# Normalisation sums by quarters of the tokens, and the hand-over from the experts to the second block, in a two-block transformer kernel

## Chip, cores and metric

The kernel runs on one core of a Trainium2 chip. The metric is the device time of one execution in microseconds (us). TensorE multiplies matrices, VectorE (DVE), ScalarE (ACT) and GpSimd (POOL) work element by element, SyncE (SP) issues the transfers from memory.

## What is computed

Two blocks, on 256 latent tokens and 256 context tokens of 1024 features, all in fp32:

```python
def first_block(x, c, ctx, ...):
    hl, hc = modulate(x, ...), modulate(ctx, ...)
    s_f, s_b = ssd_context_states(hc, lp)             # a state-space mixer, both directions
    out, _, _ = mix_stream(hl, lp, True, s_f, s_b)    # its output goes through rms_norm_gated
    x = post_norm(x, gate * out, ...)
    return post_norm(x, gate2 * hier_moe(modulate(x, ...)), ...)     # 32 experts, 2 for each token

def second_block(x, c, ctx, ...):
    for l in range(2):
        x, ctx   = post_norm_2(x, 0.5 * g1 * swiglu_2(modulate_2(x, ...))), ...     # f1i0, f1i1
        x, ctx   = post_norm_2(x, g2 * mixer(...)), ...    # l = 0: gla and latent attention; 1: neighbourhood attention
        x, ctx   = post_norm_2(x, 0.5 * g3 * swiglu_2(modulate_2(x, ...))), ...     # f2i0, f2i1

def layer_norm_2(x):
    mu = mean(x, -1);  var = mean(square(x - mu), -1)
    return (x - mu) * rsqrt(var + EPS)

def rms_norm(x, g):
    return x * rsqrt(mean(square(x), -1) + EPS) * g
```

The context is carried along until the mixer of l = 1; from there on only the 256 latent tokens are.

## The kernel before

**Layout.** Features lie on the 128 partitions, tokens along the free dimension. X is [128, 8, 512]: eight tiles of 128 features by 512 tokens, context in columns 0 to 255 and latent tokens in 256 to 511. A sum over features is thus a sum over partitions and over eight tiles, and TensorE does it: `onesD` is a 128 x 128 matrix of 1/1024, and eight fp32 matmuls against the tiles, accumulated in one PSUM bank, give the mean of each token on all 128 partitions.

**Linear layers.** Weights and inputs are split into a rounded high part and a rest (`HR`, `LR` of a weight tile `RAW`; `AH`, `AL` of an input), and a product is three matmuls: AH*HR, AL*HR, AH*LR. A weight tile is 128 x 2048 and comes through a ring of three slots; ScalarE rounds it and DVE takes the rest (`cut`). A second matrix of a feed-forward layer has its inputs in `BH`, `BL` (`BHf1i`, `BHf2i`). `linear_pe` runs the layer, output tile by output tile, and calls `after(m)` behind tile m.

**A norm.** `residual_dve` adds output tile m, times a gate, to X. `mean_pe` puts the sum of X's tile m-1 into the layer behind its output tile m; the last two sums stand behind the layer. Then come `norm_dve` (subtract the mean, eight tiles; wait for the root; reciprocal; multiply), `norm_act` (square, eight tiles; root of the variance) and `norm_pe` (eight sums of the squares, into bank 6). Behind the multiplication the lead (`lead_act`, `lead_dve`) makes AH and AL of the next layer: ScalarE applies scale and shift into `tmp` and rounds it, DVE takes the rest. The next layer's first matmul waits for the first tile of both. This form stands seven times: `out1` (256 tokens, before the routing), f1i0, `eout` (even mixer), f2i0 and f1i1 (512 tokens), `nout` (odd mixer) and f2i1 (256 tokens). ScalarE's square root needs a table load, which the program has directly behind the squares.

**Behind the experts.** The expert stage is one of two branches (`few`, at most 17 experts in use, or `every`), and its end is `after_pe`, `after_act`, `after_dve`. ScalarE waits for the context's transfer (`ctx2`), scales, shifts and rounds eight context tiles and then rounds two weight tiles (`cut(1)` takes slots 0 and 1), and only then squares for the norm `out2`. DVE adds the experts' output to X (eight), takes eight rests of the context and two of weights, and then centres. The norm's eight mean sums come with nothing beside them on TensorE.

**Small norms.** In `merge` the squares of the gated output are summed inside the z layer (16 sums, 256 tokens), and `rz`, root and reciprocal, is multiplied in 16 and more tiles later. In the even mixer the linear attention (`gla`) normalises each of four heads by a sum of one tile of 512 tokens (`omean`), and the latent attention's two inputs `ck` and `cq` (1 and 3 tiles) are normalised likewise (`cmean`), with one buffer for the squares.

**What sets the order.** Each engine has a program written out by hand, one function for each stage and engine (`ffn_act`, `gla_pe`), and does its instructions in that order. They wait for one another by named ticks on semaphores. PSUM banks are given out in order (`T.bank`) or by number (`T.hold`), and taken again when the reader frees them.

## Time and profile before

| | |
|---|---|
| median of 3 runs | 3360.7 us (3357.94 to 3367.04) |
| profiled execution | 3353.11 us |
| its span, first to last record | 3351.3 us |
| TensorE matmuls busy | 3049.3 us, 91% |
| TensorE weight loads busy | 2355.9 us, 70% |
| DVE busy | 1418.5 us, 42% |
| ScalarE busy | 1078.4 us, 32% |
| GpSimd busy | 308.4 us, 9% |
| mean granted TensorE clock | 0.959 |
| moved | 537.27 MB, mean 160 GB/s |

The rows further down come from one profiled execution. In the profile PE is TensorE, L188 the line that issues every matmul and L194 that of the transposes, L313 every ScalarE operation. Rows read "output<-inputs", buffer numbers left out; `ar`, `arf1i` and `arf2i` are the stages' scratch memories, in which squares, roots and `tmp` lie. One fp32 matmul appears as two records. Matmul records overlap, so a price is read from start to start. The chain is followed back from the last instruction, each step to what released it.

### The profile page before, as it was taken

How to read it: one execution, taken by the hardware profiler on the slowest of the kernel's cores; microseconds unless marked ns; L12 is line 12 of the kernel's file. 1: busy time of each engine (PE TensorE's matmuls, PEld its weight loads, DVE VectorE, ACT ScalarE, POOL GpSimd, SP SyncE). 2: the span in 40 equal slices, each digit the busy share in tenths (PEclk: the TensorE clock that was granted, in tenths of full speed). 3: DMA queues.
4: the chain of work that ended last, by engine and by line, in shares of the span. 5: the costliest groups of instructions: out<-in, count | busy, mean ns of one | idle time of the engine just before them, and what ended most of it. 6: DMA issues, size and time to landing. Idle time of an engine off the chain costs nothing.

```text
span 3351.3 us, 43646 instructions
## 1 busy us (share of the span) xinstructions
PE 3049.3 (91%) x18814; PEld 2355.9 (70%) x18814; DVE 1418.5 (42%) x2096; ACT 1078.4 (32%) x1579; POOL 308.4 (9%) x309
## 2 busy tenths in 40 slices
PE   6988898889999979999887888999989999897998
PEld 4866698855555548787676556878768787773998
DVE  4665454522222243333576454333243333436554
ACT  4443353312222242222432233222242121434443
POOL 0024370200000010000113001000010000300000
PEclk9988899889999989999999899999999999999999
DMA  7567755489999933232349121222222323310453
GB/s 225 161 198 234 233 163 147 150 330 396 390 391 391 398 108 97 82 109 68 94 132 319 46 76 63 91 87 95 86 82 85 104 78 98 128 62 1 138 177 101
DMA packets 415213, 537.27 MB, mean 160 GB/s; under 512 B 14340, under 2 KB 389924, under 8 KB 390308
## 3 DMA queue, kind: packets, MB, share of 16 engines
q1 hardware_dynamic: 415012, 534.38, 46.5%
q8 instruction: 151, 2.47, 0.3%
q14 instruction: 50, 0.41, 0.0%
HBM read 533.30 MB, written 1.05 MB: 159 GB/s over the span
## 4 chain that ended last, share of the span: by engine, by line
PE 82%; DVE 8%; ACT 5%; DMA 3%; issue 2%; SPq 0%; POOL 0%; DVEq 0%; ACTq 0%; POOLq 0%
PE ps L188 80%; PE ps L187 2%; DVE ar L243 2%; ACT ar L313 2%; DMA RAW<-in_ada_w 1%; DVE LR L243 1%; DVE ar L259 1%; ACT HR L313 1%; DMA RAW<-in_w_in 1%; PE ps L194 1%; DVE ar L253 0%; DVE ar L249 0%; DVE ar L262 0%; ACT arf1i L313 0%; ACT AH L313 0%
## 5 line engine op out<-in xcount | busy, mean ns | idle before, releaser
L188 PE MATMUL ps<-AH,HR 128*128 128x512 f32 (+1 forms) x2552 | 900.4, 353 | 63.3 <-DVE AL L243 40.0
L188 PE MATMUL ps<-AL,HR 128*128 128x512 f32 (+1 forms) x2552 | 886.7, 347 | 0.0
L188 PE MATMUL ps<-AH,LR 128*128 128x512 f32 (+1 forms) x2552 | 885.8, 347 | 0.0
L243 DVE TENSOR_TENSOR LR<-RAW,HR 128x2048 fp32r<-128x2048 f32 (+3 forms) x232 | 485.9, 2096 | 596.2 <-ACT HR L313 593.6
L313 ACT ACTIVATE HR<-RAW 128x2048 fp32r<-128x2048 f32 (+3 forms) x232 | 404.1, 1744 | 765.8 <-PE ps L188 664.3
L188 PEld LDWEIGHTS ps<-AH,HR 128*128 128x128 f32 x2552 | 490.1, 192 | 135.6 <-ACT arf1i L313 19.9
L188 PEld LDWEIGHTS ps<-AL,HR 128*128 128x128 f32 x2552 | 490.4, 192 | 60.0 <-issue 1.9
L188 PEld LDWEIGHTS ps<-AH,LR 128*128 128x128 f32 x2552 | 489.7, 192 | 58.9
L249 POOL TENSOR_SCALAR X<-X 128x512 f32<-128x512 f32 (+2 forms) x50 | 83.7, 1700 | 2239.7 <-ACT AH L313 1629.2
L188 PE MATMUL ps<-ar 64*128 64x128 f32 (+9 forms) x1318 | 233.5, 366 | 59.7 <-ACT ar L313 26.8
L188 PEld LDWEIGHTS ps<-ar 64*128 64x128 f32 (+2 forms) x1318 | 137.7, 186 | 137.8 <-issue 44.9
L253 DVE SCALAR_TENSOR_TENSOR X<-ps,mod,X 128x256 f32<-128x256 f32 x152 | 67.4, 479 | 313.1 <-PE ps L188 313.1
L243 POOL TENSOR_TENSOR ar<-ar 128x384 f32<-128x384 f32 (+5 forms) x138 | 151.9, 1109 | 289.9 <-DVE ar L243 115.3
L313 ACT ACTIVATE ar<-ar 128x384 f32<-128x384 f32 (+7 forms) x208 | 109.4, 557 | 158.2 <-DVE ar L249 53.7
L188 PE MATMUL ps<-BHf1i,HR 128*128 128x512 f32 x352 | 147.9, 420 | 11.6 <-DVE BLf1i L243 11.6
L313 ACT ACTIVATE ar<-ps 128x256 f32<-128x256 f32 (+4 forms) x190 | 89.1, 475 | 198.2 <-PE ps L188 189.7
L188 PE MATMUL ps<-BHf1i,LR 128*128 128x512 f32 x352 | 142.3, 404 | 0.0
L188 PE MATMUL ps<-BLf1i,HR 128*128 128x512 f32 x352 | 142.3, 404 | 0.0
L313 ACT ACTIVATE ar_few<-ps 128x512 f32<-128x512 f32 x64 | 47.0, 734 | 287.2 <-PE ps L188 287.2
L188 PE MATMUL ps<-RAW,CS 128*32 128x128 f32 x3072 | 123.3, 310 | 16.4 <-DMA RAW<-in_ada_w 8.2
L188 PE MATMUL ps<-BHf2i,HR 128*128 128x512 f32 (+1 forms) x352 | 123.6, 351 | 9.6 <-DVE BLf2i L243 9.6
L188 PE MATMUL ps<-BHf2i,LR 128*128 128x512 f32 (+1 forms) x352 | 119.6, 340 | 0.0
(182 smaller groups left out, 3748.8 us busy)
## 6 DMA issues: line engine op xcount, KB each, us to landing
RAW<-in_ada_w SPq DMA_DIRECT2D x72, 1024.0 KB, 6.4
RAW<-in_f1i SPq DMA_DIRECT2D x44, 1024.0 KB, 5.0
RAW<-in_f2i SPq DMA_DIRECT2D x44, 1024.0 KB, 5.1
RAW<-in_w_in SPq DMA_DIRECT2D x32, 1024.0 KB, 5.6
RAW<-in_w_ada SPq DMA_DIRECT2D x24, 1024.0 KB, 8.0
RAW<-in_w_eu SPq DMA_DIRECT2D x17, 1024.0 KB, 10.0
HF<-in_w_ed SPq DMA_DIRECT2D x17, 1024.0 KB, 7.8
LF<-in_w_eu SPq DMA_DIRECT2D x17, 1024.0 KB, 10.1
```

The source lines that it names most:

```text
L187: return self.e.matmul(o, w, x, start=start, stop=stop, skip_group_check=True)
L188: return self.e.matmul(o, w, x, start=start, stop=stop)
L194: return self.e.transpose(o, a, self.K.ident[sp:sp + q, sp:sp + q])
L243: return self.e.tensor_tensor(o, a, b, op) if self.e else NOTHING
L249: return self.e.tensor_scalar(o, a, s1, None, o1)
L253: return self.e.scalar_tensor_tensor(out=o, in0=a, scalar=s, in1=b, op0=o1, op1=o2) if self.e else NOTHING
L259: return self.e.reciprocal(x, x) if self.e else NOTHING
L313: return self.e.activation(o, a, f, **k) if self.e else NOTHING
```

## The change

A sum over features has a new form. `sums_pe` splits the tokens into quarters: quarter g is multiplied by 32 columns of `onesD` (now 128 x 32) into partitions 32g to 32g+31, so four matmuls with 32 weight columns and a quarter of the moving columns take the place of one with 128 columns and all tokens. The result is a 128 x n/4 tile whose row group g holds the means of quarter g. ScalarE copies it, or its root, to `stat` in SBUF, and `spread_pe` brings it back to 128 x n in a PSUM bank: four matmuls with `pick` (one matrix per quarter, with a row of ones in row 32g), one per quarter. Root and reciprocal work on n/4 columns, and DVE multiplies by the spread factor from PSUM. All norms use this, the small ones of gla, the latents and the gated norm too (there ScalarE copies the spread factor to `rz`).

Behind the experts, GpSimd scales and shifts the context into `h32` inside the expert stage (`context_pool`), and ScalarE only rounds it. One weight tile is split (`cut(0)`) in place of two, on ScalarE between the mean's copy and the squares and on DVE between the centring and the reciprocal; of the eight context rests four stand ahead of the centring and four behind. The squares of `out2` have a buffer of their own (`sq2`), `tmp2` has two tiles in place of four. The latents' squares go into `v2`, one place each, with no wait between.

```diff
 
+def sums_pe(T, K, b, x, n, first, last):
+
+    w = n // 4
+    for g in range(4):
+        r = T.mm(b[32 * g:32 * g + 32, 0:w], K.onesD[:, 0:32], x[:, g * w:(g + 1) * w], first, last)
+    return r
+
+
+def spread_pe(T, K, b, x, n):
+
+    w = n // 4
+    for g in range(4):
+        r = T.mm(b[:, g * w:(g + 1) * w], K.pick[:, g, :], x[:, 0:w], True, True)
+    return r
+
+
 def mean_pe(T, K, tag, x, n, bank=7):
 
     T.hi = 7
-    mb, held = T.hold(bank, tag, "mean")
...
         T.wait_ge(*h)
 
     def add(m):
         T.wait_ge(*K.dve.of(tag, "x", m))
-        r = T.mm(mb[:, 0:n], K.onesD[:, :], x[:, m, :], m == 0, m == 7)
+        r = sums_pe(T, K, mb, x[:, m, :], n, m == 0, m == 7)
         if m == 7:
-            r.then_inc(*K.pe(tag, "mean"))
+            r.then_inc(*K.pe(tag, "sums"))
 
...
-    vb, held = T.hold(6, tag, "var")
+    act, dve, pe = K.act, K.dve, K.pe
+    mb, held = T.hold(6, tag, "mean")
+    for h in held:
+        T.wait_ge(*h)
+    T.wait_ge(*act.of(tag, "mean row"))
+    spread_pe(T, K, mb, K.stat, n).then_inc(*pe(tag, "mean"))
+    vb, held = T.hold(7, tag, "var")
     for h in held:
         T.wait_ge(*h)
     for k in range(8):
-        T.wait_ge(*K.act.of(tag, "sq", k))
-        r = T.mm(vb[:, 0:n], K.onesD[:, :], sq[:, k, :], k == 0, k == 7)
-    r.then_inc(*K.pe(tag, "var"))
+        T.wait_ge(*act.of(tag, "sq", k))
+        r = sums_pe(T, K, vb, sq[:, k, :], n, k == 0, k == 7)
+    r.then_inc(*pe(tag, "var"))
+    rb, held = T.hold(6, tag, "factor")
+    for h in held:
+        T.wait_ge(*h)
+    T.wait_ge(*dve.of(tag, "factor row"))
+    spread_pe(T, K, rb, K.stat, n).then_inc(*pe(tag, "factor"))
     T.hi = 8
 
 
-def norm_act(S, K, tag, x, n, eps, sq, rs, post):
+def norm_act(S, K, tag, x, n, eps, sq, post, meanwhile=None):
     pe, dve, act = K.pe, K.dve, K.act
+    row = K.stat[:, 0:n // 4]
+    S.wait_ge(*pe.of(tag, "sums"))
+    S.act(row, K.ps(tag, "sums")[:, 0:n // 4], ACT.Copy).then_inc(*act(tag, "mean row"))
+    K.free(act, tag, "sums")
+    if meanwhile:
+        meanwhile()
     for k in range(8):
         S.wait_ge(*dve.of(tag, "centred", k))
         S.act(sq[:, k, :], x[:, k, :], ACT.Square).then_inc(*act(tag, "sq", k))
     S.wait_ge(*pe.of(tag, "var"))
-    S.wait_ge(*act.last)
-    S.act(rs, K.ps(tag, "var")[:, 0:n], ACT.Sqrt, bias=K.eps[:, eps:eps + 1]).then_inc(*act(tag, "root"))
+    S.act(row, K.ps(tag, "var")[:, 0:n // 4], ACT.Sqrt, bias=K.eps[:, eps:eps + 1]).then_inc(*act(tag, "root"))
     K.free(act, tag, "var")
     for k in range(8):
         post(k)
 
 
-def norm_dve(V, K, tag, x, n, rs, pre, post):
+def norm_dve(V, K, tag, x, n, pre, post, meanwhile=None):
     pe, dve, act = K.pe, K.dve, K.act
     V.wait_ge(*pe.of(tag, "mean"))
     for k in range(8):
         V.tt(x[:, k, :], x[:, k, :], K.ps(tag, "mean")[:, 0:n], SUB).then_inc(*dve(tag, "centred", k))
     K.free(dve, tag, "mean")
+    if meanwhile:
+        meanwhile()
     V.wait_ge(*act.of(tag, "root"))
+    V.rec(K.stat[:, 0:n // 4]).then_inc(*dve(tag, "factor row"))
     V.wait_ge(*dve.last)
-    V.rec(rs).then_inc(*dve())
-    V.wait_ge(*dve.last)
+    V.wait_ge(*pe.of(tag, "factor"))
     for k in range(10):
         if k < 8:
-            V.tt(x[:, k, :], x[:, k, :], rs, MUL).then_inc(*dve(tag, "normed", k))
+            V.tt(x[:, k, :], x[:, k, :], K.ps(tag, "factor")[:, 0:n], MUL).then_inc(*dve(tag, "normed", k))
+            if k == 7:
+                K.free(dve, tag, "factor")
             if pre:
...
+        self.onesD = sb("onesD", [128, 32], F32)
+        self.pick = sb("pick", [128, 4, 128], F32)
+        self.stat = sb("stat", [128, 128], F32)
...
-    for t, v in ((K.onesD[:, :], 1.0 / 1024), (K.ones[:, :], 1.0), (K.eps[:, 0:1], 1e-5), (K.eps[:, 1:2], 1e-6)):
+    for t, v in ((K.onesD[:, :], 1.0 / 1024), (K.ones[:, :], 1.0), (K.eps[:, 0:1], 1e-5), (K.eps[:, 1:2], 1e-6),
+                 (K.pick[:, :, :], 0.0)):
         G.fill(t, v).then_inc(*K.pool("constants"))
+    G.wait_ge(*K.pool.last)
+    for g in range(4):
+        G.fill(K.pick[32 * g:32 * g + 1, g, :], 1.0).then_inc(*K.pool("constants"))
+        G.wait_ge(*K.pool.last)
 
 
 def setup_act(S, K):
...
+    for w in held:
+        T.wait_ge(*w)
+    T.wait_ge(*dve.of("rz row"))
+    spread_pe(T, K, b, K.stat, 256).then_inc(*pe("rz"))
...
-    S.act(o.rz, K.ps("ssq")[:, 0:256], ACT.Sqrt, bias=K.eps[:, 0:1], scale=0.5).then_inc(*act("rz"))
+    S.act(K.stat[:, 0:64], K.ps("ssq")[:, 0:64], ACT.Sqrt, bias=K.eps[:, 0:1], scale=0.5).then_inc(*act("rz root"))
...
+    S.wait_ge(*pe.of("rz"))
+    S.act(o.rz, K.ps("rz")[:, 0:256], ACT.Copy).then_inc(*act("rz"))
+    K.free(act, "rz")
...
-    V.rec(o.rz).then_inc(*dve("rz"))
+    V.wait_ge(*act.of("rz root"))
+    V.rec(K.stat[:, 0:64]).then_inc(*dve("rz row"))
...
 
+def context_pool(G, K):
+
+    m = K.mod2[0]
+    G.wait_ge(K.loaded["ctx2"], 16)
+    for k in range(8):
+        G.ts(K.route.h32[:, k, :], K.X[:, k, 0:256], m[:, 8 + k, 1:2], m[:, k, 1:2], MUL, ADD).then_inc(K.scaled, 1)
+
+
 class Every:
 
 
...
+    context_pool(G, K)
     K.pool.note("end")
 
...
+    context_pool(G, K)
...
+        S.wait_ge(*dve.of("out2", "normed", k))
         if k > 1:
-            S.wait_ge(*dve.of("f1i0h", v, k - 2))
-        tb = K.tmp2[:, i, :]
-        S.act(tb, K.X[:, k, s:s + 256], ACT.Identity, scale=m2[:, 8 + k, v:v + 1],
-              bias=m2[:, k, v:v + 1]).then_inc(*act())
+            S.wait_ge(*dve.of("f1i0h", 0, k - 2))
+        S.act(tb, K.X[:, k, 256:512], ACT.Identity, scale=m2[:, 8 + k, 0:1], bias=m2[:, k, 0:1]).then_inc(*act())
         S.wait_ge(*act.last)
-        S.act(K.AH[:, k * 512 + s:k * 512 + s + 256], tb, ACT.Copy).then_inc(*act("f1i0h", "hi", k))
-        act.note("f1i0h", v, k)
-
-    def post(k):
-        S.wait_ge(*dve.of("out2", "normed", k))
-        half(k, 256, 0, 2 + k % 2)
-
-    for k in range(8):
-        half(k, 0, 1, k % 2)
-    S.cut(1)
-    norm_act(S, K, "out2", o.XL, 256, 0, o.h32, o.rs, post)
+        S.act(K.AH[:, k * 512 + 256:k * 512 + 512], tb, ACT.Copy).then_inc(*act("f1i0h", "hi", k))
+
+    norm_act(S, K, "out2", o.XL, 256, 0, o.sq2, post, lambda: S.cut(0))
     act.note("lead end")
 
 
...
-        half(k, 0, 1, k % 2)
-    V.cut(1)
-    norm_dve(V, K, "out2", o.XL, 256, o.rs, ("ln2g", "ln2b"), lambda k: half(k, 256, 0, 2 + k % 2))
+    def context(k):
+        at = slice(k * 512, k * 512 + 256)
+        V.wait_ge(*act.of("f1i0h", 1, k))
+        V.tt(K.AL[:, at], o.h32[:, k, :], K.AH[:, at].bitcast(F32), SUB).then_inc(*dve("f1i0h", 1, k))
+
+    def meanwhile():
+        for k in range(4, 8):
+            context(k)
+        V.cut(0)
+
+    def latents(k):
+        at = slice(k * 512 + 256, k * 512 + 512)
+        V.wait_ge(*act.of("f1i0h", "hi", k))
+        V.tt(K.AL[:, at], K.tmp2[:, k % 2, :], K.AH[:, at].bitcast(F32), SUB).then_inc(*dve("f1i0h", "lo", k))
+        dve.note("f1i0h", 0, k)
+
+    for k in range(4):
+        context(k)
+    norm_dve(V, K, "out2", o.XL, 256, ("ln2g", "ln2b"), latents, meanwhile)
     dve.note("lead end")
 
...
 
+    def factor(hd):
+        T.wait_ge(*dve.of("ofactor row", hd))
+        spread_pe(T, K, bank("ofactor", hd), o.rss[hd], 512).then_inc(*pe("ofactor", hd))
...
-        T.mm(bank("omean", hd)[:, :], K.onesD[:, :], o.sqs[hd % 2], True, True).then_inc(*pe("omean", hd))
...
+            factor(hd - 1)
+    factor(3)
     pe.note("gla end")
 
...
-        S.act(o.rss[hd % 2], K.ps("omean", hd)[:, :], ACT.Sqrt, bias=K.eps[:, 1:2],
+        S.act(o.rss[hd], K.ps("omean", hd)[:, 0:128], ACT.Sqrt, bias=K.eps[:, 1:2],
               scale=8.0).then_inc(*act("oroot", hd))
...
 
+    def onorm(hd):
+        V.wait_ge(*pe.of("ofactor", hd))
+        then(V.stt(o.oT[:, hd, :], o.oT[:, hd, :], K.v("gng"), K.ps("ofactor", hd)[:, :], MUL, MUL))
+        K.free(dve, "ofactor", hd)
...
-        rs = o.rss[hd % 2]
         V.wait_ge(*act.of("oroot", hd))
...
         if hd < 2:
...
+    onorm(3)
     dve.note("gla end")
...
+        r.then_inc(*pe("cmean", i))
+
+    def factor(i):
+        b = bank("cfactor", i)
+        T.wait_ge(*dve.of("cfactor row", i))
+        spread_pe(T, K, b, o.P[0][:, 128 * i:128 * i + 128], 512).then_inc(*pe("cfactor", i))
+
+    factor(0)
+    factor(1)
     j, w = T.weights("ukv", None, 0, 1, 0, 1024, False)
...
-        if i:
-            S.wait_ge(*dve.of("cnorm", 0))
-        S.act(o.P[0], K.ps("cmean", i)[:, :], ACT.Sqrt, bias=K.eps[:, 1:2], scale=w).then_inc(*act("croot", i))
+            S.act(o.v2[:, i + m, :], x[:, m, :], ACT.Square).then_inc(*act("csq", i, m))
+    for i, w in enumerate((8.0, 1024.0 / 384)):
+        S.wait_ge(*pe.of("cmean", i))
...
 
+    for i in range(2):
+        V.wait_ge(*act.of("croot", i))
...
-        then(V.rec(o.P[0]))
+        V.wait_ge(*pe.of("cfactor", i))
         for m in range(nt):
-            then(V.stt(x[:, m, :], x[:, m, :], K.v(key, m), o.P[0], MUL, MUL), "cnorm", i)
+            then(V.stt(x[:, m, :], x[:, m, :], K.v(key, m), K.ps("cfactor", i)[:, :], MUL, MUL), "cnorm", i)
+        K.free(dve, "cfactor", i)
     V.take()
     for hd in range(4):
```

**ScalarE, from the end of the expert branches to the lead of f1i0.** `tmp` is the context, or the latent tokens, scaled, `ar<-X` the squares and `ar<-ps,eps` the root. Before:

```order
L313 ACTIVATE tmp<-X,mod 128x256
L313 ACTIVATE AH<-tmp 128x256
L313 ACTIVATE HR<-RAW 128x2048 x2
L313 ACTIVATE ar<-X 128x256 x8
L313 ACT_TABLE_LOAD
L313 ACTIVATE ar<-ps,eps 128x256
L313 ACTIVATE tmp<-X,mod 128x256
L313 ACTIVATE AH<-tmp 128x256
```

(The first two rows are the last of eight such pairs.) Now, with `ar` the context as GpSimd has scaled it, and `ar_all<-X` the squares:

```order
L313 ACT_TABLE_LOAD
L313 ACTIVATE AH<-ar 128x256 x8
L313 ACTIVATE stat<-ps 128x64
L313 ACTIVATE HR<-RAW 128x2048
L313 ACTIVATE ar_all<-X 128x256 x8
L313 ACT_TABLE_LOAD
L313 ACTIVATE stat<-ps,eps 128x64
L313 ACTIVATE tmp<-X,mod 128x256
L313 ACTIVATE AH<-tmp 128x256
```

The eight scalings and one weight tile have gone from the front of the squares, and the other weight tile now stands behind the copy of the mean.

**DVE, the same place.** `X<-ps,mod,X` adds the experts' output, `AL` rows are the rests of the context, `X<-X,ps` first the centring. Before:

```order
L253 SCALAR_TENSOR_TENSOR X<-ps,mod,X 128x256 x8
L243 TENSOR_TENSOR AL<-tmp,AH 128x256 x8
L243 TENSOR_TENSOR LR<-RAW,HR 128x2048 x2
L243 TENSOR_TENSOR X<-X,ps 128x256 x8
L259 RECIPROCAL ar<-ar 128x256
L243 TENSOR_TENSOR X<-X,ar 128x256
```

Now:

```order
L253 SCALAR_TENSOR_TENSOR X<-ps,mod,X 128x256 x8
L243 TENSOR_TENSOR AL<-ar,AH 128x256 x4
L243 TENSOR_TENSOR X<-X,ps 128x256 x8
L243 TENSOR_TENSOR AL<-ar,AH 128x256 x4
L243 TENSOR_TENSOR LR<-RAW,HR 128x2048
L259 RECIPROCAL stat<-stat 128x64
L243 TENSOR_TENSOR X<-X,ps 128x256
```

Four rests of the context and the one weight rest have moved behind the centring, the second weight rest is gone from here.

**TensorE, from the last layer rows of f1i0's second matrix to the first of the even mixer.** `arf1i` are the squares, AH*HR begins the next layer. Before:

```order
L188 MATMUL ps<-BHf1i,HR 128x512
L188 MATMUL ps<-BLf1i,HR 128x512
L188 MATMUL ps<-BHf1i,LR 128x512
L188 MATMUL ps<-X,onesD 128x512 x2
L188 MATMUL ps<-arf1i,onesD 128x512 x8
L188 MATMUL ps<-AH,HR 128x512
```

Now:

```order
L188 MATMUL ps<-BHf1i,HR 128x512
L188 MATMUL ps<-BLf1i,HR 128x512
L188 MATMUL ps<-BHf1i,LR 128x512
L188 MATMUL ps<-X,onesD 32x128 x8
L188 MATMUL ps<-stat,pick 128x128 x4
L188 MATMUL ps<-arf1i,onesD 32x128 x32
L188 MATMUL ps<-stat,pick 128x128 x4
L188 MATMUL ps<-AH,HR 128x512
```

Each sum has become four small ones, and two spreads have come in: one between the mean's sums and the squares', one between the squares' and the next layer.

## Rows read from the trace of the kernel before

**Rows 1.** The page, chain that ended last, shares of the span by engine

```profile
PE 82%; DVE 8%; ACT 5%; DMA 3%; issue 2%; SPq 0%; POOL 0%; DVEq 0%; ACTq 0%; POOLq 0%
```

**Rows 2.** Chain, behind f1i0 and even mixer; columns: start us, us, what

```profile
1620.87 1.14 PE ps L188 x2
...
1623.43 7.15 PE ps L188 x16
...
1631.33 3.36 DVE arf1i L259
...
1638.07 19.15 PE ps L188 x72
...
2053.00 8.81 PE ps L188 x16
```

**Rows 3.** Chain, behind the experts

```profile
1210.51 3.23 DVE X L253 x8
...
1219.85 1.81 ACT HR L313
...
1223.96 2.28 DVE LR L243
...
1234.83 0.43 DVE X L243
...
1238.10 6.97 PE ps L188 x17
```

**Rows 4.** Chain, end of linear attention and the latents

```profile
1886.35 0.69 ACT ar L313
...
1896.86 0.64 ACT ar L313
...
1906.50 30.37 PE ps L188 x90
```

**Rows 5.** Timeline, TensorE: start us, us, what; sums inside 512-, then 256-token layers

```profile
1572.46 1.02 PE L188 MATMUL ps<-X,onesD 128*128 128x512 f32 x2
...
1573.55 0.39 PE L188 MATMUL ps<-BLf1i,HR 128*128 128x512 f32 x1
...
627.14 0.59 PE L188 MATMUL ps<-X,onesD 128*128 128x256 f32 x2
...
627.69 0.28 PE L188 MATMUL ps<-AL,HR 128*128 128x256 f32 x1
```

**Rows 6.** Timeline, TensorE, a conditioning job inside a layer

```profile
113.28 1.08 PE L188 MATMUL ps<-RAW,CS 128*32 128x128 f32 x32
...
114.63 0.40 PE L188 MATMUL ps<-AL,HR 128*128 128x512 f32 x1
```

**Rows 7.** Groups of instructions, ScalarE, the copy of a conditioning row

```profile
L313 ACT ACTIVATE mrow<-ps 128x128 f32<-128x128 f32 x96 | 26.2, 273 | 111.6 <-PE ps L188 95.3 <-DMA X<-in_ctxT 16.0
```

**Rows 8.** Timeline, TensorE, transposes in the routing

```profile
664.55 3.31 PE L194 MATMUL ps<-ident,ar 128*128 128x128 f32 x16
```

**Rows 9.** Timeline, ScalarE, table loads behind f1i0 and behind nout

```profile
1627.64 1.28 ACT L313 ACT_TABLE_LOAD   x1
...
3131.23 1.28 ACT L313 ACT_TABLE_LOAD   x1
```

**Rows 10.** Chain, reciprocal of the 256-token norm nout

```profile
3133.30 1.76 DVE ar L259
```

**Rows 11.** DMA issues in 655 to 700 us; last column: us to landing

```profile
X<-in_ctx2T SPq DMA_DIRECT2D x1, 1024.0 KB, 28.1
```

**Rows 12.** Timeline, ScalarE, first weight tile in f1i0

```profile
1248.70 1.92 ACT L313 ACTIVATE HR<-RAW 128x2048 fp32r<-128x2048 f32 x1 [2.33 <-POOL X L249]
```

**Rows 13.** Timeline, ScalarE, roundings for the layer ya

```profile
522.57 4.90 ACT L313 ACTIVATE AH<-ar,vec 128x256 fp32r<-128x256 f32 x12
```

**Rows 14.** Engines by stretch: busy us of PE, PEld, DVE, ACT, POOL; granted clock

```profile
1638.00:1644.00 6.00, 5.93 (x15) 4.74 (x16) 6.00 (x8) 5.87 (x12) 6.00 (x4) 0.54 0.00 0
```

More of the change, by code:

```diff
@@ L1485, in post @@
               bias=mod[:, 24 + k, 0:1]).then_inc(*act("h32", k))
-    norm_act(S, K, "out1", o.XL, 256, 0, o.sq, o.rs, post)
+    norm_act(S, K, "out1", o.XL, 256, 0, o.sq, post)
     for q in range(2):
@@ L1501, in route_dve @@
     meet(V, K, "out1 end")
-    norm_dve(V, K, "out1", o.XL, 256, o.rs, ("ln1g", "ln1b"), None)
+    norm_dve(V, K, "out1", o.XL, 256, ("ln1g", "ln1b"), None)
     for j in range(2):
@@ L2652, in gla_dve @@
             read(hd + 1)
-        rs = o.rss[hd % 2]
         V.wait_ge(*act.of("oroot", hd))
-        then(V.rec(rs))
-        then(V.stt(o.oT[:, hd, :], o.oT[:, hd, :], K.v("gng"), rs, MUL, MUL), "onorm", hd)
-        then(V.tt(o.oT[:, hd, :], o.oT[:, hd, :], o.r[:, hd, :], MUL))
+        V.rec(o.rss[hd]).then_inc(*dve("ofactor row", hd))
         if hd < 2:
@@ L2660, in gla_dve @@
                 pass
+        if hd:
+            onorm(hd - 1)
+    onorm(3)
     dve.note("gla end")
@@ L2888, in latent_dve @@
     meet(V, K, "even out")
-    norm_dve(V, K, "eout", K.X, 512, o.rs, None, lead_dve(V, K, o.lead))
+    norm_dve(V, K, "eout", K.X, 512, None, lead_dve(V, K, o.lead))
     dve.note("even end")
@@ L3010, in odd_act @@
     meet(S, K, "odd out")
-    norm_act(S, K, "nout", o.XL, 256, 1, o.sq, o.rs, lead_act(S, K, o.lead, "nout"))
+    norm_act(S, K, "nout", o.XL, 256, 1, o.sq, lead_act(S, K, o.lead, "nout"))
     act.note("odd end")
@@ L3057, in odd_dve @@
     meet(V, K, "odd out")
-    norm_dve(V, K, "nout", o.XL, 256, o.rs, None, lead_dve(V, K, o.lead))
+    norm_dve(V, K, "nout", o.XL, 256, None, lead_dve(V, K, o.lead))
     dve.note("odd end")
```

71 lines of the change are left out of this document (34 added, 37 removed).

## Prediction

> **What bounds the kernel now.** I read the page's chain of waits first: 82% of the span is TensorE work that follows other TensorE work [rows 1]. The reader is to see there that only two kinds of edit can pay: less work on TensorE inside its dense stages, and shorter hand-overs where it stands still. Then I took the chain, in order of time, around the places that the diff touches. It shows the hand-over of a 512-token norm: last sum of the mean, eight matmuls for the variance, root, reciprocal, first matmul of the next layer, 17.2 us from 1620.87 to 1638.07 [rows 2]. The kernel has four of these (behind f1i0, even mixer, f2i0, f1i1), three for 256 tokens on the path of the same shape (out1, nout, f2i1), a 256-token one behind the experts with more work ahead of it [rows 3], and the small norms at the end of the linear attention [rows 4]. The matmuls of the sums, which also stand inside the dense stages, were read from the timeline [rows 5].
>
> **Price of a sum.** Inside a linear layer one 512-token sum costs 1573.55 - 1572.46 less an ordinary step of 0.23 = 0.86 us, a 256-token one 627.69 - 627.14 less 0.12 = 0.43 us [rows 5]. The new form (weights of 32 columns, 128 moving columns, four column groups) already runs in the conditioning jobs. 32 records, eight rounds of four, last 1.08 us, of which the last one's own duration is some 0.27, so a round is about 0.11 us; from the first of them to the second matmul of the layer behind is 1.35 us, so leaving the form costs 1.35 - 8 x 0.11 - 0.24 = about 0.23 us [rows 6]. Entering isn't priced by a row; I take 0.1. A new sum of 512 tokens is two rounds, 0.22 + 0.33 = 0.55 us: 0.31 to 0.36 saved. With six sums inside each of four layers (the last two stand behind it) that is 24 x 0.33 = **7.9 us saved**. For 256 tokens the rounds have 64 columns, between half a round's price and all of it: 0.44 to 0.55 against 0.43. There are 18 of those in three layers and 15 in the z layer: 33 x 0.05 = **1.6 us lost** (0 to 4).
> The Trainium skill (TensorE: Matmul & The Clock Gate, Measured speedup vs the span model) has three column tiles at 2.38 times one, not 3, which speaks against a full fourfold. By it a round would be 0.14 us and the saving some 2 us smaller; the row above shows four at the full rate, and I go by the row.
>
> **The 512-token norm.** Seven sums of the mean hide behind layer and DVE as before, so only the last one counts: 1.14 us become about 0.45. New behind it are a copy to SBUF of 128x128, as the mrow copies, 0.27 us [rows 7], and four matmuls that spread the rows, eight records with full weights. Transposes of that size take 3.31 / 16 = 0.21 us each at the half clock [rows 8], so 0.1 at the full one, and a spread is 1.1 to 1.9 us with its tail. The squares thus start 0.45 + 0.3 + 1.1 - 1.14 = 0.75 us later. They come 0.6 apart and a new sum takes 0.25 to 0.45, so the variance no longer ends last: behind the eighth square ScalarE loads the root's table, 1.28 us from 1627.64 [rows 9], hidden before and now the bound. Root from 1627.64 + 0.75 + 1.30 = 1629.7. Root on 128 columns 0.3; reciprocal by the two sizes seen, 3.36 at 512 and 1.76 at 256 [rows 2, 10], 6.25 ns a column, so 0.96 at 128: 1631.0. Spread at either clock: 1632.1 to 1632.9, where before the first scaling stood at 1631.33 + 3.38 = 1634.71. Saved 1.8 to 2.6, I take 2.2. Behind the even mixer the variance took 8.81 us, not 7.15 [rows 2]; that goes too: 3.9. **Together 3 x 2.2 + 3.9 = 10.5 us saved** (8 to 13).
>
> **The 256-token norms.** Here the change has little to take away: before, the table load ended at 3131.23 + 1.28 = 3132.51 [rows 9] and the root followed within 0.3 us. The mean costs 0.45 + 0.25 + 1.1 against 0.71, so all is 1.1 us later; root -0.2, reciprocal 1.76 to 0.56 [rows 10], second spread 1.1 to 1.9. Net 0.5 to 1.3 us later each, **2.7 us lost** in three.
>
> **Behind the experts.** Before: from 1210.51 ScalarE scales and rounds the context (9.3 us), rounds two weight tiles, DVE takes their rests, and the norm's scaling starts at 1234.83 [rows 3]. After: GpSimd did the scaling long before, in the expert stage, where it has next to nothing to do; the context's transfer, issued as that stage begins, takes 28.1 us [rows 11], against over 500 that the stage lasts. ScalarE has eight roundings (2.8 us), done before DVE's last residual at 1213.7. Sums done 1214.2, row 1214.5, spread 1215.6, centred 1215.7 to 1218.4, squares until 1219.1 (the rounding of one weight tile, 1.9 us, lies ahead of them, beside spread and centring). DVE goes on with four rests (1.4) and one weight tile (2.29): 1222.2, which is later than table load and root (1220.7), so this ends last. Reciprocal of 64 columns 0.56, spread 1.9: 1224.7, **10.1 us earlier**. Given back: the second weight tile is no longer ready. ScalarE meets GpSimd's last scaling, 10.6 us behind the first matmul (1248.70 against 1238.10) [rows 3, 12], then rounds the tile (1.9) and DVE takes the rest (2.3 + 0.2): TensorE gets it at +15.0. It has used up the first tile of 48 matmuls at 48 x 0.23 + 2.3 (half of 5 us, the half clock as now) = +13.3: 1.7 us of wait (1 to 4 if the clock is full). Net **8.4 us saved** (5.5 to 10).
>
> **End of the linear attention.** TensorE takes on four spreads and loses four sums; up to the third head's root (1886.35) that nets to +0.3 us, since one spread fits there. Then, instead of reciprocals of 3.36 in a row until 1896.86 [rows 4], DVE has 0.96 each and four products of 1.5: the last ends about 1893.0, 3.8 earlier. Behind it four squares no longer wait for a matmul each (one buffer before: 9.6 us from 1896.86 to 1906.50); the sums end at 1896.3, reciprocals 1896.8 and 1897.8, first spread at half clock 1898.9, first product 1899.7. There TensorE starts the ukv products, which it did behind the last sum, 1906.50 and 1.9 for two halves at the half clock: 1908.4. From there it is busy as before until 1936.9 [rows 4], but cold for some 3 us that it was not: 8.6 - 1.6 = **7.0 us saved** (5 to 8.5).
>
> **The gated norm** in the merge stage: TensorE spreads behind the gates (1.1 us), ScalarE copies it (0.4), and only then come the roundings from 522.57 [rows 13], for which the next layer waits: **1.0 us lost**. The constants' extra fills on GpSimd stand at the program's start, beside the transfer of TensorE's first weights: nothing, and 2 us should they be late.
>
> **Sum.** 7.9 - 1.6 + 10.5 - 2.7 + 8.4 + 7.0 - 1.0 = 28.5 us less. The profiled execution took 3353.1 us (3351.3 span), and would take 3324.6; it lies 7.6 under the median of the runs, so against the median of 3360.7 I say 3332.
>
> **Rivals.**
> Quarters in a row, the case on the slower side. If the four groups of a sum do not run side by side, because they read slices of one tile and not four weights, a sum is eight records in turn. 512 tokens: 8 x 0.11 + 0.33 = 1.2 us, 24 x 0.35 = 8 lost in place of 7.9 saved; 256: 0.8 to 1.2 against 0.43, about 18 lost. The variance becomes the bound again: 512 norms save 5, 256 ones lose 5, experts and attention save 12 together. Net 15 slower, 3376. It decides from about 0.9 us a sum. For it: no row has this operand; against it: the same form in [rows 6].
> Issue as the limit is its milder kin: a fixed price for each small matmul, whatever its columns. With twice the price per record that the row shows (1.08 / 32 = 0.034), sums of 512 would gain nothing, those of 256 lose 0.4 each: 28.5 - 7.9 - 12 = 9 faster, 3352. The Trainium skill (TensorE: Matmul & The Clock Gate, Back-to-back issue gap) knows such a floor, 62 ns a matmul with hardware decode off; 32 in 1.08 us speak against it here.
> Colder. In the stretch behind a norm TensorE is at half clock already for most of 6 us (granted 0.54) [rows 14]. With light sums in place of seven dense microseconds the clock may fall earlier and return later: 1.7 us more at each of six restarts, and up to 4 of wait for the second tile: 17 faster, 3344.
> Warmer. The standstill shrinks from 7.5 us to some 3.3 behind the spread; if the clock then holds, four or five leads gain 1.5 each (the lead's roundings on ScalarE allow no more): 35 faster, 3326.
>
> **Chances.** Forecast 0.58, colder 0.18, warmer 0.13, issue 0.05, quarters in a row 0.06. Range: the forecast's own bounds are 3321 to 3343; with colder and warmer and a median that moves by 4 from run to run, 3316 to 3347 leaves out no more than 0.2. A measurement tells 0.3% (10 us) from no change: faster 0.88, same 0.06, slower 0.06.
>
> **What would show it.** Records of a sum: eight in under 0.5 us. In f1i0's norm the table load directly ahead of the root, reciprocal below 1.1 us. DVE's weight rest as releaser ahead of the reciprocal behind the experts, and TensorE waiting for a DVE weight rest some 13 us into f1i0. Ukv products some 8 us sooner after the attention's last read. If sums inside layers cost over 0.8 us, or the clock stays low through a lead's first 10 us, the forecast is wrong.

## The result, and the profile after

The changed kernel takes 3349.4 us (median of 10, 3344.6 to 3358.0) against 3363.3 (10 runs, 3357.3 to 3371.7): ratio 0.9962, 95% interval 0.9951 to 0.9972. That is 13 us faster by the ratio, where 28.5 were forecast; the time lies above the range (3316 to 3347). Run once more beside other executions of the kernel before it came out at 0.9974 (0.9963 to 0.9985).

The page's chain has nearly the shares of [rows 1]:

```profile
PE 81%; DVE 8%; ACT 5%; DMA 3%; issue 2%; SPq 0%; POOL 0%; DVEq 0%; ACTq 0%; POOLq 0%
```

**A sum inside a layer** (timeline of TensorE, start us, us, what; the place of [rows 5]). The layer's matmuls come 0.23 apart, the one ahead of the sum starts at 1572.05, so the sum costs 1573.08 - 1572.05 - 2 x 0.23 = 0.57 us, where it was 0.86:

```profile
1572.38 0.42 PE L188 MATMUL ps<-X,onesD 128*32 128x128 f32 x8
...
1573.08 0.40 PE L188 MATMUL ps<-BLf1i,HR 128*128 128x512 f32 x1
```

**The norm behind f1i0** (chain; the rows answer to the first four of [rows 2]):

```profile
1618.78 0.47 PE ps L188 x8
...
1619.27 0.29 ACT stat L313
...
1619.60 1.17 PE ps L188 x8
...
1621.52 4.82 ACT arf1i L313 x8
...
1626.35 1.28 ACT L313
...
1627.65 0.38 ACT stat L313
...
1628.05 0.96 DVE stat L259
...
1629.15 2.06 PE ps L188 x8
...
1634.65 18.68 PE ps L188 x72
```

Every step that was forecast is there in its order: copy, spread, squares, the table load directly ahead of the root, a reciprocal of 0.96 us. From the mean's last sum to the next layer it is 15.87 us in place of 17.20: 1.33 saved, not 2.2. The missing part is the second spread, 2.06 us and 0.14 ahead of it, at the half clock (granted 0.50), where 1.1 to 1.9 was forecast; up to the root the forecast holds within 0.1 us.

**Behind nout** (chain; [rows 10] is its reciprocal before):

```profile
3113.01 1.09 PE ps L188 x8
...
3119.77 1.96 PE ps L188 x8
...
3121.82 0.43 DVE X L243
...
3123.36 0.43 DVE AL L243
...
3127.12 0.43 DVE AL L243
3127.55 0.34 DVE X L243
3127.89 0.04 issue
3127.93 22.13 PE ps L188 x160
```

AL of the first tile is ready at 3123.8, but TensorE starts at 3127.93, and what releases it is no AL but a multiplication of X: the eighth. Bank 6, in which the factor lies, is freed behind it, and the next layer's first step takes four banks at once, bank 6 among them. No step of the forecast has this wait.

**Behind the experts** (chain; answers to [rows 3]):

```profile
1223.47 2.40 DVE X L243 x7
1225.87 1.34 DVE AL L243 x4
1227.21 2.20 DVE LR L243
1229.42 0.47 DVE stat L259
1229.89 0.14 issue
1230.03 1.96 PE ps L188 x8
...
1234.87 0.33 DVE AL L243
...
1241.02 0.34 DVE X L243
1241.37 0.04 issue
1241.41 20.79 PE ps L188 x80
```

DVE's rests stand ahead of the reciprocal, as forecast, and again the eighth multiplication (1241.02) releases TensorE, 6.2 us behind the first tile's AL (ready at 1235.20). One forecast sign is missing: from its start on TensorE works for 48 us without a wait, and none for a weight rest stands 13 us into f1i0.

**End of the linear attention** (chain; answers to [rows 4]):

```profile
1886.42 0.38 ACT ar L313
...
1892.93 2.45 ACT ar L313 x5
...
1896.51 32.25 PE ps L188 x104
```

The third head's root (1886.42) stands where it stood before (1886.35), so the times compare as they are: the products are through by 1892.9 (1893.0 forecast), the squares go in one piece.

### The profile page after: what moved, and what is told of

It reads as the page before. It is cut to its first block, busy times and chain, and to the rows that moved or that the text cites. A ratio compares the mean times of both kernels' runs of the same rounds, so it can differ in the third digit from the quotient of the medians.

```text
span 3347.2 us, 45837 instructions
## 1 busy us (share of the span) xinstructions
PE 3048.3 (91%) x19910; PEld 2360.1 (71%) x19910; DVE 1382.0 (41%) x2096; ACT 1071.8 (32%) x1580; POOL 313.7 (9%) x322
## 4 chain that ended last, share of the span: by engine, by line
PE 81%; DVE 8%; ACT 5%; DMA 3%; issue 2%; SPq 0%; POOL 0%; DVEq 0%; ACTq 0%; POOLq 0%
PE ps L188 79%; PE ps L187 2%; DVE ar L243 2%; ACT ar L313 2%; DMA RAW<-in_ada_w 1%; DVE LR L243 1%; ACT HR L313 1%; DMA RAW<-in_w_in 1%; ACT arf1i L313 1%; DVE ar L259 1%; PE ps L194 1%; DVE X L243 1%; ACT L313 1%; DVE ar L253 0%; DVE AL L243 0%
## 5 line engine op out<-in xcount | busy, mean ns | idle before, releaser
L313 ACT ACTIVATE ar<-ps 128x512 f32<-128x512 f32 (+4 forms) x191 | 89.6, 475 | 207.8 <-PE ps L188 198.3
L188 PE MATMUL ps<-BLf2i,HR 128*128 128x512 f32 (+1 forms) x352 | 120.8, 343 | 0.0
```

The source lines that it names most:

```text
L188: return self.e.matmul(o, w, x, start=start, stop=stop)
L313: return self.e.activation(o, a, f, **k) if self.e else NOTHING
```

## Experiments

Where a number below is a stretch "from the last residual" or "to the first residual", it is read from start to start of the same DVE or TensorE instructions in one trace of each kernel. Medians are of 4 to 12 executions, and ratios are to the kernel before in the same sitting.

**The kernel before, again.** No edit.

> The kernel before, once more, to have its granted clock over several executions and a second profile. In the two profiles at hand the changed kernel is 5.5 us later in the state-space stage (from 193 to 395 us), 3.5 later in the linear attention (1645 to 1840) and 4.3 later in the odd mixer (2863 to 3106), places whose code the change does not touch, and the executions of the changed kernel all have a mean granted clock of 0.943 to 0.948 against 0.959 in the one profile of before. Theory A (luck of one execution): the kernel before has clocks of 0.945 to 0.955 in most executions, its second profile is 3358 to 3370 us long, and the stage from 193 to 395 is 2 us or more longer than in the first profile. Theory B (the change makes TensorE colder everywhere): all executions of before are at 0.956 to 0.962 and the second profile repeats the first within 2 us in each of the three stages.

Median 3362.5, ratio 0.9993 (0.9984 to 1.0002); profiled span 3362.2 at a granted clock of 0.954. The state-space stage took 189.9 us in place of 187.4, the odd mixer 245.1 in place of 242.5. Mostly theory A: the profile on which the forecast rests was about 9 us shorter than the kernel's usual execution. That explains nothing of the miss in the medians beyond what the forecast read out of this one trace (see the even mixer's norm below), but comparisons with that one trace would mislead, so the stretches below use both, and that of before_context where its code is the old one.

**Another first bank behind out2 and nout.**

```diff
     spread_pe(T, K, rb, K.stat, n).then_inc(*pe(tag, "factor"))
     T.hi = 8
+    if tag in ("out2", "nout"):
+        T.bi = 6
```

> The changed kernel, with the PSUM rotation set on by a few places behind the norms out2 and nout, so that the next layer's first four banks are 7, 0, 1, 2 and bank 6, in which the spread factor lies until DVE has multiplied the eighth tile, comes later. Theory A (bank 6 is what these two layers wait for): TensorE's first matmul behind nout comes directly behind the first rest of the input, some 4 us sooner, at 4.0 us behind the end of the factor's spread less than the present 6.4, and behind out2 some 6 us sooner. Since TensorE then goes at the pace of the tiles of its input (0.94 us each in nout, 1.46 in out2), about 3 and 5 us of it stay: 8 us faster than the changed kernel, ratio to before 0.9938. Theory B (the wait is for the input tiles or the weights): no change, 0.9962.

Median 3344.2, ratio 0.9939 (0.9927 to 0.9951). TensorE's waits in the stretch behind nout (engine, line, waited for: us in total, times, longest), first of the changed kernel, then of this one:

```profile
PE ps L188 <- DVE X L243: 6.2, 1, 6.2
```

```profile
PE ps L188 <- ACT ar L313: 2.2, 1, 2.2
```

Theory A holds for the wait: nout's next layer starts 12.22 us behind the last residual in place of 16.21. Behind the experts the start came 4.1 us sooner (17.48 for 21.60) but up to f1i0's first residual only 0.7 of it was left. The first AL came 1.9 us later here (17.3 us behind the last residual, 15.4 in the changed kernel), so the wait that went was the full 6.2; then TensorE waits 1.2 us for the second weight tile's rest. And the shifted rotation put f2i0 and the odd mixer behind bank 6, 7 us later each (23.65 for 16.56, 23.49 for 16.39).

**The table load ahead.**

```diff
+    S.act(K.stat[:, 0:1], K.ones[:, 0:1], ACT.Sqrt).then_inc(*act())
+    S.wait_ge(*act.last)
     S.wait_ge(*pe.of(tag, "sums"))
```

> The changed kernel, with one square root of a single column on ScalarE ahead of its wait for the mean's sums in each of the eight norms, so that the root's table is loaded there and not between the eighth square and the root. Theory A (the table load ends last there, as forecast): the root comes 0.6 to 0.9 us sooner in the four norms of 512 tokens and 0.5 in those of 256, none behind the experts, where DVE's weight rest ends last: 4.5 us faster than the changed kernel, ratio to before 0.9949. Theory B (the sums of the squares end just as late): root at the same time, no change, 0.9962.

Median 3351.6, ratio 0.9964 (0.9950 to 0.9978): no gain. Chain behind f1i0:

```profile
1625.84 4.88 PE ps L188 x64
...
1630.74 0.38 ACT stat L313
```

Now the sums of the squares end last. The root comes 9.32 us behind the last pair of residuals in place of 9.80: half a microsecond a norm, not 0.6 to 0.9. So the forecast had the right bound (the table load), with the next one right behind it.

Why the median gains nothing can be read as well. In three of the eight norms (out1, eout, nout) ScalarE isn't idle long enough ahead of the mean's last sum, and the load stands in front of the mean's copy. Behind the even mixer (timeline of ScalarE):

```profile
2043.64 1.28 ACT L313 ACT_TABLE_LOAD   x1 [11.02 <-DVE X L253]
...
2045.17 0.28 ACT L313 ACTIVATE stat<-ps 128x128 f32<-128x128 f32 x1
```

The copy comes 2.1 us behind the last residual in these three, where it came at 0.9 to 1.0, and the root 0.4 to 1.3 us later than in the changed kernel. The stretch from out1 to the experts is 1.9 us longer. The one behind the experts is 2.9 longer too, but there the mean's sums come late, at a colder clock.

**Matmuls to hold the clock.**

```diff
         r = sums_pe(T, K, vb, sq[:, k, :], n, k == 0, k == 7)
+        if k < 7:
+            idle_pe(T, K, 1)
     r.then_inc(*pe(tag, "var"))
+    idle_pe(T, K, 3)
...
     spread_pe(T, K, rb, K.stat, n).then_inc(*pe(tag, "factor"))
+    idle_pe(T, K, 7)
```

> The changed kernel, with matmuls whose result nobody reads on TensorE (128 columns of fp32 weights, 256 moving columns, 0.43 us at the full clock): one behind each square's sums, three ahead of the factor's spread, seven behind it. They compute nothing of the reference. Theory A (colder: the light sums and the idle time behind them let the clock fall before the spreads and the restart, and this costs about 1 us in each factor spread and 2 in each restart): the factor's spread takes 1.1 us in place of 2.06, the next layer starts with full clock in most norms, 10 us faster than the changed kernel, ratio to before 0.993. Theory B (the clock falls and returns as it did before whatever fills the gap, or ScalarE's pace of the input tiles hides it): within 3 us of the changed kernel, or slower by what the extra matmuls push back (1 to 2 us a norm), 0.996 to 0.999.

Median 3377.2, ratio 1.0043 (1.0026 to 1.006): slower by far more than either theory had. Chain behind f1i0:

```profile
1628.59 10.29 PE ps L188 x84
...
1638.95 1.14 PE ps L188 x8
```

The clock does what theory A says: the factor's spread takes 1.14 us, not 2.06. But eight sums with an idle matmul between them, and three behind, take 10.3 us where the sums alone took 4.84. What a restart at full clock gives back doesn't show: from f1i0's norm to the rounding of a weight tile 200 us on it is 198.85 us, against 197.3 to 201.2 in the other kernels, so 2 us would be lost among them. The largest losses are at the end of f2i1 (25.5 us for 17.55) and behind the experts (172.9 for 166.4). What the colder clock costs in f1i0's norm is 0.9 us in a spread, and this way to it costs more than it gives.

**The rotation for all norms.**

```diff
+    if 2 <= T.bi <= 5:
+        T.bi = 6
```

> The changed kernel, with the PSUM rotation set on behind every norm after which bank 6 would be among the next layer's first four banks. In the kernel with the rotation set on behind out2 and nout alone, the start behind nout came 4.0 us sooner, but the shifted rotation put f2i0's and the odd mixer's first banks on bank 6: from the last residual to the first matmul 23.65 and 23.49 us in place of 16.56 and 16.39. Theory A (the bank decides and what is lost there is not made up): all starts as in the changed kernel or sooner, the two at 16.4 again, nout's at 12.2: some 10 us faster than that kernel less what it made up, 3335 to 3338 us, ratio 0.991 to 0.992. Theory B (a later start is made up by inputs that are then all ready): the ratio stays at 0.994.

Median 3345.4, ratio 0.9940 (0.9927 to 0.9953). f2i0 and the odd mixer start at 15.65 and 16.40 again, nout's next layer at 12.22. The median did not fall below after_bank's all the same, and the traces don't support theory B for it. From the even mixer's last residual to f2i0's first one the late start had cost its full length (168.5 us, 161.7 here). In this kernel's trace 6.4 us are lost elsewhere, from f1i0's last residual to the even mixer's first (388.2 us against 381.8), a stretch that lies between 380.2 and 388.2 in all kernels with the new attention norms. For the odd mixer it is open: 264.6 us here and 261.5 with the late start, but kernels with the early one lie anywhere between 257 and 266.

**Old form for out1, nout and f2i1.**

```diff
+def whole(tag, n):
+    return n == 256 and tag != "out2"
...
+        if whole(tag, n):
+            r = T.mm(mb[:, 0:n], K.ones[:, 0:128], x[:, m, :], m == 0, m == 7)
+        else:
             r = sums_pe(T, K, mb, x[:, m, :], n, m == 0, m == 7)
```

> The changed kernel, with the norms of 256 tokens out1, nout and f2i1 in their old form (sums with all 128 weight columns, root and reciprocal on 256 columns of each partition, no spread; the factor 1/1024 is applied by the centring and the root). Theory A (these three lose in the new form what the traces show: out1 1.7 us, nout with the stretch behind it 7.8, f2i1 at the end 1.7): 11 us faster than the changed kernel, 3338, ratio 0.993. Theory B (the losses there are luck of one profile or come from elsewhere): ratio 0.996.

Median 3336.8, ratio 0.9914 (0.9901 to 0.9928): 16 us by the ratios, more than theory A had. nout's hand-over takes 10.52 us (16.21), f2i1's end 15.9 (17.55), out1's way to the experts 566.4 (567.6). Two more pieces lie where nothing was changed: the two places in f2i1 where its second matrix takes over. Engines by stretch there (busy us of PE, PEld, DVE, ACT, POOL, the granted clock, DMA share, GB/s), of the changed kernel, then of this one:

```profile
3198.00:3207.00 9.00, 7.07 (x47) 6.90 (x46) 3.03 (x4) 2.59 (x4) 0.00 (x0) 0.81 0.44 126
3294.00:3303.00 9.00, 7.07 (x47) 6.90 (x47) 2.91 (x5) 2.47 (x4) 0.00 (x0) 0.81 0.48 134
```

```profile
3182.00:3191.00 9.00, 7.07 (x61) 6.90 (x60) 4.52 (x6) 2.98 (x5) 0.00 (x0) 1.00 0.37 106
3278.00:3287.00 9.00, 7.07 (x61) 6.90 (x60) 3.83 (x5) 3.24 (x4) 0.00 (x0) 1.00 0.45 133
```

TensorE is busy for the same time, but at a granted clock of 0.81 and not 1.00, and 47 matmuls are done in it and not 61.

**The experts' hand-over alone, on the kernel before.**

```diff
+def few_pool(G, K):
+    context_pool(G, K)
...
-    S.cut(1)
-    norm_act(S, K, "out2", o.XL, 256, 0, o.h32, o.rs, post)
+    norm_act(S, K, "out2", o.XL, 256, 0, o.sq2, o.rs, post, lambda: S.cut(0))
```

> The kernel before with the experts' hand-over alone changed: GpSimd scales the context in the expert stage, ScalarE rounds it, one weight tile is split between in place of two ahead; sums and norms in their old form, so no spread and no bank 6 held behind the norm. Theory A (the hand-over is worth what was forecast, 8.4 us less about 1 for the old sums): from the experts' last residual to the first residual of f1i0 (172.9 us before, 166.4 in the changed kernel) some 165 us; ratio 0.9975 to 0.998. Theory B (the second weight tile, split later, gives it back): above 170 us, ratio 0.999 to 1.

Median 3353.0, ratio 0.9960 (0.9946 to 0.9975): this part alone is worth as much as the whole change (0.9962), and the stretch is shorter than either theory had. From the last residual to f1i0's first one it takes 160.3 us, against 172.9 before and 166.4 in the changed kernel. Its chain:

```profile
1224.83 2.21 DVE LR L243
...
1227.13 1.76 DVE ar L259
...
1230.96 11.70 POOL X L249 x8
...
1242.82 1.93 ACT HR L313
...
1244.86 2.30 DVE LR L243
1247.17 0.14 issue
1247.30 14.77 PE ps L188 x64
```

A reciprocal of 1.76 and no spread, and TensorE starts 13.65 us behind the last residual (24.83 before, 21.60 changed). Then comes the wait that was forecast: GpSimd's scalings, ScalarE's rounding of the second weight tile, DVE's rest, TensorE at 1247.30.

**Both.**

> The kernel mixed with the rotation set on behind norms as in bank_all. In mixed only out2 and the four norms of 512 tokens hold bank 6 behind them. Theory A (only out2 is then behind bank 6, and its wait is mostly hidden by the wait for the second weight tile): 0 to 2 us faster than mixed, ratio 0.9925 to 0.993. Theory B (the waits for bank 6 cost their full length): 5 us or more faster than mixed, below 0.992.

The edits of mixed and bank_all together. Median 3328.7, ratio 0.9897 (0.9882 to 0.9912). Behind the experts 163.8 us (167.3 in mixed), so more than theory A's 0 to 2, less than B's 5; the rest is within the intervals.

**All norms of 256 tokens in the old form.** `whole` returns n == 256.

> The changed kernel, with every norm of 256 tokens in its old form, out2 behind the experts too, and the PSUM rotation set on behind the norms of 512. What differs from mixed_bank is out2 alone. Behind the experts the kernel before_context (new hand-over, old norm) went from the last residual to f1i0's first residual in 160.3 us, the changed kernel in 166.4, mixed_bank in 163.8. Theory A (out2's own norm loses in the new form too, and the new hand-over is worth 12 us and not 8 without it): that stretch 160 to 161 us, 3 us faster than mixed_bank, 3325, ratio 0.9888. Theory B (the second weight tile, which comes at the same time either way, decides): stretch 163 to 164 us, ratio 0.9897.

Behind the experts 160.4 us, as theory A has it: out2's norm alone, in its new form, costs 3.4 us there. The median, 3329.7, ratio 0.9897 (0.9882 to 0.9912), doesn't show them.

**The second weight tile ahead of GpSimd.**

```diff
     norm_act(S, K, "out2", o.XL, 256, 0, o.sq2, post, lambda: S.cut(0))
+    S.cut(1)
```

(and the same on DVE)

> The kernel best, with the second weight tile split directly behind the lead's roundings on ScalarE and its rests on DVE, ahead of the wait for GpSimd's eight scalings of X (11.7 us) that begins f1i0 on ScalarE. Theory A (TensorE's wait for the second tile, which mixed_bank's chain has between the lead and the matmul at 1248.07, is the end of that wait): the tile is ready 2 to 3 us sooner, 2.5 us faster than best, ratio 0.988. Theory B (something else keeps the first matmuls of that tile): no change.

Median 3325.4, ratio 0.9886 (0.9871 to 0.9902), the lowest of all, though within the intervals of best and mixed_bank. The GpSimd step has gone from the chain, which goes from the lead straight into TensorE:

```profile
1230.48 0.35 DVE AL L243
1230.82 0.14 issue
1230.96 31.25 PE ps L188 x129
```

The stretch is 159.3 us, 1.1 less and not 2.5; the rows don't show where the rest went.

**With the table load ahead, for 512 tokens alone.**

```diff
     if not w:
+        S.act(K.stat[:, 0:1], K.ones[:, 0:1], ACT.Sqrt).then_inc(*act())
```

> The kernel best_cut, with a square root of one column ahead of the wait for the mean's sums in the four norms of 512 tokens. In after_table the root came 9.32 us behind the last pair of residuals in place of 9.80, the last sum of the squares then ending last. Theory A (this holds in each of the four, and what after_table lost, it lost around out1, whose way to the experts was 2 us longer there): 1.9 us faster than best_cut, ratio 0.9875. Theory B (no gain, as in after_table's median): ratio as best_cut.

Median 3326.9, ratio 0.9888 (0.9873 to 0.9903). The hand-overs are 15.8 to 15.9 us in three of the four norms (16.05 to 16.5 without) and 17.98 behind the even mixer (15.70 without), where the load again stands ahead of the mean's copy. So what three norms gain, 1.3 us together, the fourth takes back: theory B.

**The attention's small norms in the old form.** `gla_*` and `latent_*` as in the kernel before, on the kernel best.

> The kernel best, with the norms of the linear attention's heads and of the two latents in their old form (sums with 128 weight columns, reciprocals of 512 columns, one buffer for the latents' squares; the factor 1/1024 sits in the root). Theory A (the new form there is worth what the traces show, 9 us up to the first ukv product and up to 3 more behind it, where 7.0 were forecast): 9 to 12 us slower than best, ratio 0.9915 to 0.9925. Theory B (the 2 us over the forecast are luck of the clock in the profiles): 7 us slower, ratio 0.991.

Median 3335.6, ratio 0.9913 (0.9900 to 0.9927): 5.4 us slower than best by the ratios, below both theories, though intervals of some 5 us each way leave room for either. Up to the first ukv product it takes 73.8 us against 63.5, 10 us more, so the local gain is as large as theory A says, and 9.7 of it are left at the even mixer's first residual. The largest difference the other way is in the next stretch: 161.0 us against 164.6 in best, where the other kernels without a late start have 161.6 to 162.5. So best's one profile is long there; where the medians lose the rest is not shown.

**The changed kernel, again.**

> The changed kernel once more. By stretches of the traces the change gives 20 us (sums inside layers 7.7, four norms of 512 tokens 5.3, attention 9.1, experts 6.5, less 8.4 in the norms of 256 tokens and 0.7 in the gated norm), the medians give 14. Theory A (the missing 6 us are luck of the clock in the one profile, in stretches that the change does not touch, such as 193 to 395 us, the linear attention before its last norm, and the first layers of f2i1): a second profile has these at the values of the other kernels (f2i1's first half 77.5 to 78 us and not 80.1), and the ratio comes out at 0.994 to 0.9955. Theory B (the changed kernel pays for it in these places each time): f2i1's first half 80 us again, ratio 0.9955 to 0.997.

Median 3354.8, ratio 0.9974 (0.9963 to 0.9985): theory B. f2i1's first half is 79.9 us again (80.0; 77.9 before), its second hand-over 64.73 (64.76; 63.3, 64.8 and 63.3 in three profiles with the old norms), the odd mixer 248.7 (248.1).

## Why the prediction was wrong

By its own steps, in us of the trace; minus is faster.

| step | forecast | measured | from |
|---|---|---|---|
| 24 sums of 512 tokens in layers | -7.9 | -7.8 | last tiles of f1i0: 54.71 to 52.76, six sums |
| 33 sums of 256 tokens | +1.6 | -0.5 to -0.9 | z layer, first to last sum, 50.72 to 50.67 and 50.23 (two profiles), out1 and nout 0.1 each, f2i1 27.46 to 27.21 |
| four norms of 512 | -10.5 | -5.3 | 17.73 to 16.4; eout 17.87 to 16.6 (15.6 in the second profile) |
| three norms of 256, with what follows them | +2.7 | +12 | out1 +1.0, nout +5.7, f2i1 +2.1 and +1.5, end +1.65 |
| experts' hand-over | -8.4 | -6.5 | 172.9 to 166.4 |
| end of the attention | -7.0 | -9.0 | 73.3 to 64.3 (means of three and of two profiles) |
| gated norm | +1.0 | +0.8 | last sum to first rounding for ya: 46.85 to 47.63 |
| sum | -28.5 | about -16.5 | medians: -13.9, and -7.2 in the second sitting |

**Right.** The price of a sum: eight records of a sum last 0.42 us, and over a layer a sum saves 0.32 (0.31 to 0.36 forecast). Quarters in a row and issue as the limit are out: two rounds of four end 0.42 us behind the first one's start, and the last record alone lasts 0.27 of that. The Trainium skill (TensorE: Matmul & The Clock Gate, Measured speedup vs the span model) has three column tiles at 2.38 times one; an estimate by it, 0.14 us a round, has a sum save some 0.25. The measured 0.32 is nearer to the full rate, but the 0.07 between them is less than the 0.1 that was assumed, and never priced, for entering the form, so the layers alone don't decide it. The shape of the norm, the attention's new order and the price of the gated norm came out as worked out. The wait for the second weight tile exists too, 1.2 us where 1.7 was forecast, and ends 15.1 us into the layer (15.0 forecast), but only once the wait for the bank is gone.

**The step that failed** is the 256-token norms, "net 0.5 to 1.3 us later each", and with it the experts. The hand-over itself was mis-sized little: up to the first multiplication nout's norm is 1.7 us longer, since the second spread with the way to it takes 2.2 us and not 1.1 to 1.9. The largest missing piece is a wait that the change adds: the factor is multiplied out of PSUM, so its bank stays held until the eighth tile, and behind out2 and nout that bank is among the next layer's first four. I followed who waits for the reciprocal, and not who waits for the bank. It costs 4.0 us behind nout. Behind the experts it costs 6.2 at the start (4.1 between the two traces) and 0.7 at f1i0's first residual, since TensorE then goes at the pace of its inputs and waits for the second weight tile; but the larger loss there is the new norm itself: with the old norms the same hand-over gives 12.6 us and not 6.5, and with out2's norm alone changed back 3.4 come back. The forecast put the hand-over and the new norm of out2 into one term and so hid that one takes back a quarter to a half of the other. Of the +12, the 3.6 inside f2i1 are a loss without a known way (below).

**The 512-token norms** are a term mis-sized by half. The variance no longer ends last, and the table load does, both as forecast. The spread, put at 1.1 to 1.9 (1.5 in the sum), is 2.2 with the way to it, which is 0.7 of the 0.9 that each norm lacks; the first spread came as forecast (table load 0.80 us later than before, 0.75 forecast). For eout the 8.81 us of [rows 2] were an outlier: the second profile of the kernel before has that hand-over at 17.87 us and not 19.57, so 1.7 of its 3.9 us of saving was never there.

**Colder** was given 0.18, with its price in the restarts. The clock did fall earlier. Engines by stretch behind f1i0, first of the changed kernel, then of the second profile of the kernel before at the same place:

```profile
1622.00:1628.00 6.00, 4.84 (x64) 1.61 (x64) 3.67 (x7) 5.97 (x10) 0.00 (x0) 0.50 0.01 3
```

```profile
1624.00:1632.00 8.00, 6.56 (x16) 2.95 (x16) 4.87 (x8) 6.10 (x9) 0.00 (x0) 1.00 0.00 0
```

But in the restart it is as cold as before (0.58 from 1634 to 1640, against 0.54 in [rows 14]), and the loss is in the spread, about 0.9 us for each, and, it seems, in the two places of f2i1. Behind the experts it is larger. The same place, in after_bank and in before_context:

```profile
1217.00:1223.00 6.00, 4.17 (x72) 3.55 (x72) 2.54 (x8) 2.42 (x4) 0.00 (x0) 0.50 0.03 7
```

```profile
1218.00:1224.00 6.00, 5.04 (x24) 4.12 (x23) 5.62 (x17) 4.89 (x11) 0.00 (x0) 1.00 0.01 3
```

In the first 5 us behind the last residual the granted clock is 0.50 to 0.79 in all eight profiles with out2's new norm, and 1.00 in all five with the new hand-over and the old norm. The first spread, forecast to end 2.3 us behind the last residual, ends at 3.0 and 3.3 where the clock is 0.78 or 0.79, and at 4.5 to 5.3 where it is 0.50 or 0.51. So the forecast's rival was right in part, at a place that it didn't name.

**Open** is why TensorE falls to the half clock at the two places of f2i1: of six profiles with the new 256-token norms in all six at the second and in four at the first (not in bank_all and after_warm), of nine with the old ones in two at the second and in none at the first. So it goes with those norms; the way is not shown. Open too is what the difference between some -16.5 of the steps and the -7 to -14 of the medians consists of. The state-space stage (187.4 to 193.2 us in profiles with old code, 189.6 to 192.9 with new) and the odd mixer vary by 3 to 6 us from one profile to the next, and so does the way from f1i0's norm to the even mixer's first residual (389.9, 395.3 and 397.5 us in the kernels with the old attention norms and f1i0's old one; 380.2 to 388.2 in the eleven profiles with both new). That is as large as what is missing.

## What to carry to other kernels

When an operand moves from SBUF to PSUM, list who takes that bank next and when its last reader lets go; a bank rotation makes that a different layer in each place, and setting it on by hand (two lines) was worth 7 to 8 us by the ratios. A shorter form of a reduction pays where columns are many: with 512 tokens it saved 1.3 us a norm, with 256 it lost 1.7 or more, since two more passes over TensorE cost nearly the same in both (1.17 and 2.06 us against 1.09 and 1.96). Before moving a table load ahead of a wait, look whether the engine is idle there for longer than the load. Cost a hand-over and a norm inside it apart, even if one change brings both.

## What was not expected of the hardware

- 64 small matmuls with 32 weight columns keep TensorE busy for 4.84 of 6 us, and the granted clock is 0.50; sixteen dense fp32 records, 6.56 of 8 us, keep it at 1.00. The stretches ahead differ too (busy 3.75 of 6 us at 1616 to 1622, against 5.89 of 6 at 1618 to 1624), so which of the two lets the clock fall is not shown.
- An idle matmul of 256 columns behind each sum of quarters brought eight sums from 4.84 us to over 9 (84 records in 10.29 us, of which the last three idle matmuls are six).
- The kernel before has a granted clock of 0.959 in one profile and 0.954 in another, and single stages differ by 2.5 to 5.4 us between them, without a change in code.
